# Compress products of the sample sequences' pages: fp32 products replaced by three one-pass products of high and low parts

## What is computed

```
def compress(rows, pe, w1, w2):
    ...
    chunks = rows[:, :n_chunks * CMP_STRIDE].reshape(b, n_chunks, CMP_STRIDE, g, dh)
    ...
    w1_parts = w1.reshape(r, CMP_STRIDE * dh, CMP_HIDDEN)
    pre = pe.reshape(-1) @ w1
    for m in range(r):
        pre = pre + jnp.einsum("bngf,fh->bngh", chunks[:, m:m + n_cmp], w1_parts[m])
    return jax.nn.gelu(pre) @ w2

def nsa_sample(...):
    kcc = compress(history(pool_ck, kc), pe[0], w1[0], w2[0])
    vcc = compress(history(pool_cv, vc), pe[1], w1[1], w2[1])
    o_cmp, p = cmp_attention(q, kcc, vcc, pos)
    idx, ok = select_blocks(p, pos, n_slc)
    ...  # selected_attention over the 16 best blocks, window_attention over the last 512 rows
```

## Time and profile before

| | us |
|---|---|
| median of 3 runs | 1987.12 (1981.58 to 1989.87) |
| the profiled execution, its own time | 1985.21 |
| its span, first to last instruction | 1983.6 |
| PE busy | 1827.7 (92%) |
| DVE, ACT, POOL busy | 898.8, 610.4, 369.0 |
| attention of the prompt, 8 rounds | about 925 to 1116 of the span |
| the four pairs | 1116.8 to 1487 of the span |

### The profile page before, as it was taken

The page is one execution under the profiler, slowest core; times in us unless marked ns, Lnnn a source line. Parts: engine busy times, 40 slices in busy tenths (PEclk is TensorE's granted clock), DMA queues, the critical chain, the costliest instruction groups (busy, mean ns, idle before and its releaser), DMA issues. The chain is left out here.

```text
span 1983.6 us, 33847 instructions
## 1 busy us (share of the span) xinstructions
PE 1827.7 (92%) x12814; PEld 1560.1 (79%) x12814; DVE 898.8 (45%) x1320; ACT 610.4 (31%) x1073; POOL 369.0 (19%) x580
## 2 busy tenths in 40 slices
PE   8999787999999998997888999998988799999996
PEld 8999667999999988995555444444448799999996
DVE  3353287444544434225777340404046644544434
ACT  3222223333332222233666421212123333333222
POOL 0004414000000220020000435343433200000122
PEclk9999679999999998996999999999998899999998
DMA  6222021222223322250000377676643122222331
GB/s 266 85 74 65 28 75 57 91 91 85 85 84 90 89 83 107 85 164 1 1 1 1 97 243 241 222 258 211 212 137 110 56 94 85 85 90 89 88 88 46
DMA packets 89322, 206.15 MB, mean 104 GB/s; under 512 B 13289, under 2 KB 50698, under 8 KB 88466
## 3 DMA queue, kind: packets, MB, share of 16 engines
q1 hardware_dynamic: 71426, 145.00, 22.8%
q0 software_dynamic: 16800, 54.76, 8.3%
q10 hardware_dynamic: 1008, 5.16, 0.6%
HBM read 188.10 MB, written 16.76 MB: 103 GB/s over the span
## 5 line engine op out<-in xcount | busy, mean ns | idle before, releaser
L1230 PE MATMUL ps<-x_parts,piece_parts 128*128 128x272 f32 x6528 | 838.3, 291 | 42.8 <-DVE x_parts L1819 35.0
L1230 PEld LDWEIGHTS ps<-x_parts,piece_parts 128*128 128x128 f32 x6528 | 830.8, 191 | 48.2 <-issue 26.0
L1618 DVE TENSOR_TENSOR piece_parts<-ring,piece_parts 128x1024 fp32r<-128x1024 f32 (+1 forms) x200 | 244.4, 1222 | 617.4 <-ACT piece_parts L1449 617.4
L1449 ACT ACTIVATE piece_parts<-ring 128x1024 fp32r<-128x1024 f32 (+1 forms) x200 | 208.6, 1043 | 584.6 <-PE ps L1230 563.0
L1230 PE MATMUL ps<-big_parts,piece_parts 128*128 128x272 f32 x2176 | 337.2, 291 | 10.6 <-DVE big_parts L1098 6.6
L1230 PEld LDWEIGHTS ps<-big_parts,piece_parts 128*128 128x128 f32 x2176 | 299.9, 192 | 11.9 <-issue 6.8
L659 PE MATMUL ps<-slots,big 128*128 128x512 f32 x512 | 223.9, 595 | 1.6 <-POOLq L1122 1.4
L659 PEld LDWEIGHTS ps<-slots,big 128*128 128x128 f32 x512 | 96.0, 190 | 119.5 <-issue 117.8
L1230 PE MATMUL ps<-hidden_parts,piece_parts 128*128 128x272 f32 x704 | 145.2, 288 | 0.0
L1230 PEld LDWEIGHTS ps<-hidden_parts,piece_parts 128*128 128x128 f32 x704 | 110.7, 189 | 0.0
L1954 POOL COPY slots<-slots 128x2 f32 (+1 forms) x44 | 21.5, 488 | 463.0 <-ACT slots L1578 463.0
(11 more groups left out here) (299 smaller groups left out, 1716.6 us busy)
## 6 DMA issues: line engine op xcount, KB each, us to landing
ring<-in_w_up SPq DMA_DIRECT2D x88, 512.0 KB, 3.3
ring<-in_w_in SPq DMA_DIRECT2D x48, 512.0 KB, 3.4
ring<-in_w_down SPq DMA_DIRECT2D x32, 512.0 KB, 3.5
slots<-in_cmp_k SPq DMA_DIRECT2D x128, 128.0 KB, 3.0
slots<-in_cmp_v POOLq DMA_DIRECT2D x128, 128.0 KB, 2.5
slots<-in_slc_k SPq DMA_DIRECT2D x128, 128.0 KB, 4.1
slots<-in_slc_v POOLq DMA_DIRECT2D x96, 128.0 KB, 2.6
ring<-in_w_out SPq DMA_DIRECT2D x16, 512.0 KB, 3.4
```

The lines of the kernel that those rows point to most:

```text
L1230: mm = pe.matmul(ps[:, 2 * psum_set + h, 0:HT], split[:, slot % 2, w_part, k * 128:(k + 1) * 128], rhs(k)[v_part][:, h * HT:(h + 1) * HT], ...
L1449: act.activation(split[:, s % 2, 0, 0:size], raw[s][:, 0:size], ACT.Copy).then_inc(w_hi, 1)
L1618: ve.tensor_tensor(split[:, s % 2, 1, 0:size], raw[s][:, 0:size], as_f32(split[:, s % 2, 0, 0:size]), ALU.subtract).then_inc(w_lo, 1)
```

## The change

- **compress**: for every chunk column c (8 in each compress), the page rows of 128x512 are divided. ACT copies them to one of four buffers `chunk_hi` in fp32r (`high`), DVE subtracts and writes the low part over the rows in their slot (`low`). PE makes 6 one-pass products: w1_h and w1_l times high for both parts, then w1_h times low for both parts. It waits for `chunk_high` ahead of the first and for `chunk_low` ahead of the fifth. ACT waits for `chunk_free`, which PE raises with the fifth product of a chunk, and which starts at 4. ACT takes over the wait for the pages (`slot_in`).
- **w1** is divided once, in 8 pieces of 128x512, one in each round of the prompt's attention: ACT's copy after ta(3), DVE's subtraction at the round's end. The high part is put where `xls` lay. So DVE first adds `xhs` and `xls` to one row of x in each round (`whole_row`, 128x544), and the layer norm after `out1` reads that sum (one instruction of DVE for a row instead of two). PE waits for `w1_lo` ahead of the first compress.
- **PE's order**: cv0 is cut at chunks 4 and 6 instead of by parts. Chunks 0 to 3 stand after k20, 4 and 5 after k21, 6 and 7 after sc.
- ACT's 32 and DVE's 32 new instructions in a pair are spread by hand between the old ones.
- The buffers lie where the first piece of `out1`, the gate weights and the prompt's masks lay. DVE's loop over the pairs is now three rounds and one written out.

The diff, cut to its core:

```diff
+            pe.sem_inc(chunk_free, 4)
-                    for part in parts:
-                        dst = ps[:, 2 * b + part, :].rearrange("p (g pg n) -> p pg g n", g=4, pg=NPG)
-                        for c in range(8):
-                            mm = pe.matmul(dst, w1[:, v, (part * 8 + c) * 128:(part * 8 + c + 1) * 128], rows[:, :, c, :, :],
-                                           start=c == 0, stop=c == 7)
+                    for c in cs:
...
+                        pe.wait_ge(chunk_high, n)
+                        for part in range(2):
+                            pe.matmul(dst[part], w1_h[:, v, wc[part]], high, start=c == 0, stop=False)
+                            pe.matmul(dst[part], w1_l[:, v, wc[part]], high, start=False, stop=False)
+                        pe.wait_ge(chunk_low, n)
+                        pe.matmul(dst[0], w1_h[:, v, wc[0]], low, start=False, stop=c == 7).then_inc(chunk_free, 1)
+                        mm = pe.matmul(dst[1], w1_h[:, v, wc[1]], low, start=False, stop=c == 7)
...
-                        compress(1, 0, (0,))
+                        compress(1, 0, range(4))
+                compress(1, 0, range(4, 6))
...
-                compress(1, 0, (1,))
+                compress(1, 0, range(6, 8))
...
+                    if u == 3:
+                        act.wait_ge(x_whole, R + 1)
+                        act.activation(w1_h_pieces[:, bass.ds(R, 1), :], w1_pieces[:, bass.ds(R, 1), :], ACT.Copy).then_inc(w1_hi, 1)
...
+            def high(r, name, *cs):
...
+                for c in cs:
+                    if c == 0:
+                        act.wait_ge(slot_in[sl], 384 * r + 256 if sl == 3 else 256 * (1 + 2 * r))
+                    act.wait_ge(chunk_free, 32 * r + (CHUNKS[name] + c + 1))
+                    act.activation(chunk_hi[c % 4], rows[:, c, :, :], ACT.Copy).then_inc(chunk_high, 1)
...
+                high(r, "ck0", *range(8))
+                high(r, "ck1", 0, 1, 2, 3)
+                first(0, ("ck1", 4, 5))
+                high(r, "ck1", 6, 7)
+                high(r, "cv0", 0, 1, 2, 3)
                 first(1)
+                high(r, "cv0", 4, 5, 6, 7)
+                high(r, "cv1", 0, 1)
...
+                high(r, "cv1", 2, 3)
                 first(2)
+                high(r, "cv1", 4, 5)
...
+                high(r, "cv1", 6)
...
+                high(r, "cv1", 7)
                 first(3)
...
+                ve.wait_ge(w1_hi, R + 1)
+                ve.tensor_tensor(w1_l_pieces[:, bass.ds(R, 1), :], w1_pieces[:, bass.ds(R, 1), :],
+                                 as_f32(w1_h_pieces)[:, bass.ds(R, 1), :], ALU.subtract).then_inc(w1_lo, 1)
+                if not last:
+                    whole_row(R + 1)
...
+            def low(r, name, *cs):
+                low_rows, rows = chunk_rows(slots_low, name), chunk_rows(span(F, SLOTS_AT, 4 * 4096), name)
+                for c in cs:
+                    ve.wait_ge(chunk_high, 32 * r + (CHUNKS[name] + c + 1))
+                    ve.tensor_tensor(low_rows[:, c, :, :], rows[:, c, :, :], as_f32(chunk_hi[c % 4]), ALU.subtract).then_inc(chunk_low, 1)
...
-                    ve.scalar_tensor_tensor(out=half(y[:, m, :]), in0=half(as_f32(xhs[:, m, :])), scalar=float(ALPHA), in1=pset(m),
+                    whole = x_rows if r == 2 else as_f32(xhs)
+                    ve.scalar_tensor_tensor(out=half(y[:, m, :]), in0=half(whole[:, m, :]), scalar=float(ALPHA), in1=pset(m),
```

## The result

The changed kernel takes 1960.49 us (median of 4 executions, 1958.39 to 1965.89) against 1984.35 (1981.04 to 1989.87) before: a ratio of 0.9879, 95% interval 0.9856 to 0.9901. That is 24 us less. The forecast was 1942.5, or 44.6 us less; the time lies in the range of 1930 to 1964, at its upper end. The profiled execution took 1962.13 us with a span of 1960.5, so 23.1 us less than the one before. One execution of a later run (the kernel before with one edit) took 3594 us where its five others took 1964 to 1973, and is left out of its figures. About half of the expected gain is missing, and this part is about where it went.

A forecast was written before the change was run, and what follows sets the result against it. PE was taken as the bound, over half of each pair being compress products. Terms -55.4 + 1.4 - 3.4 + 2.8 (ranking) + 3.4 + 2.0 + 4.6 = -44.6 us took 1985.2 to 1940.6; 1.9 for the median gave 1942.5, range 1930 to 1964.

The forecast's parts named there:

- The products: Compress products in the four pairs: 192 one-pass products of 0.2165 us replace 128 of 0.433 a pair, -55.4 us.
- stalls at cv1: PE waits for cv1's chunks 6 and 7, 0.5 and 0.3 us a pair: +3.4 us for four (0 to +5).
- weight loads show: Rival, chance 0.08: a compress product takes 0.225 us, as one-pass products show 12 ns more; kernel at 1949 us.
- Kcc's wait: PE's 0.85 us wait ahead of sc is filled by two chunks of cv0: -3.4 us for four pairs.
- Start of pair 0: ACT's table load now stands ahead of the first chunk copy, so PE starts later: +1.4 us.
- The pages: PE reaches slc_k's loads behind J sooner and may wait: 0 to 2.4 us a pair, 0.5 taken, +2.0 us.
- second rival: Pages late, chance 0.10: DMA engines set slc_k's end, 2.4 us a pair, +7.6 on the forecast, 1950 us.
- The prompt's attention: DVE's two new instructions at each round's end delay the next round: 0.65 us at seven boundaries, +4.6 us (+2.5 to +10).
- Behind cv1: From cv1's end all stays as it was, with the same DMA wait of about 3 us for slc_v.
- The low parts beside POOL: Rival, chance 0.07: DVE's subtractions slow to 1.67 us beside POOL for half the chunks, +24 us, 1966 us.
- PE at its lower clock for all compress products: Rival, chance 0.03: waits idle PE often enough that its clock falls, 166 us on top, 2109 us.
- 131 ns a product: Rival, chance 0.01: compress products come closer than one column a tick, pairs lose 66 us more, 1877 us.

The follow-up runs named there:

- the kernel before with one edit: Kernel before the change, its slc_v products waiting for the other sample's half only ahead of the ninth of sixteen steps: median 1970.7 us, ratio 0.9918.
- divided wait and late window: Changed kernel, waiting for slc_v's second half only before the ninth step, and issuing the window's loads behind cv0's chunk 3: 1945.81 us, ratio 0.9805.

## Why the prediction was right and wrong, point by point

- **The number.** 1960.49 lies in the range, 18 us above the forecast, and partly by luck: the high end of 1964 was added up from 6.5 us for the product's price, 7.6 for the pages, 5.4 for the prompt and some clock, while the product's price alone cost 13.1. Pairs came 83.8 to 88.2 us apart, not 79 to 80.
- **The products: the term that was mis-sized.** Forecast -55.4 us with 0.2165 us for a product (and +3.4 for stalls at cv1, so -52.0); measured -36.6. 768 x (0.2335 - 0.2165) = 13.1 us are the product's price alone; the low clock at pair 0's start adds 2.7, and the first product of each of the twenty stretches takes 0.1 us more, some 2 in all; fewer stalls at cv1 give 2.2 back. The step that failed is the reading of the earlier trace rows: 0.125 us for 272 columns was split into one column a tick and "12 ns that look like a weight load". Read as a price per column, 0.46 ns, it gives 0.235 us for 512, within 1% of what came. Both readings fit the one row; I wrote the additive one down as the upper bound, 0.225. The rival *weight loads show* named too small a price and the wrong cause. The pass of 0.2165 us in the earlier trace rows is half of a two-pass product, and that isn't a one-pass product.
- **cv1's stalls** are 0.3 us a pair, not 0.85. The low clock at pair 0's first products I had not counted.
- **Kcc's wait** went as said: -3.8 for -3.4. **Start of pair 0**: +1.4 as said; 2.81 us of waiting in place of 1.40.
- **The pages.** The forecast left open whether issue (31.7 us after the pair's start) or the DMA engines (38.6) set their end, and took 0.5 of at most 2.4 us a pair. It was the engines: L730 started 38.9 to 40.2 us after the start. My reason for the small 0.5 was the step that failed here. I took the share of 0.77 early in the pair for room, but later in the same stage the engines of the kernel before were full:

```profile
1323.90:1326.90 3.00, 3.00 (x8) 1.33 (x7) 0.00 (x0) 0.00 (x0) 2.84 (x5) 1.00 1.07 364
1329.90:1332.90 3.00, 3.00 (x8) 1.33 (x7) 0.00 (x0) 1.12 (x1) 0.00 (x0) 1.00 1.02 379
```

  From J to cv1 the sum was +4.8, it measured +9.1, between the forecast and its second rival (+12.4). The ranking did run on under the wait, as said, which capped it; what the cap left out is the lower clock behind the longer idle time, 5.7 us in L730 (L743, the window's scores, gets 1.5 us of such a loss back).
- **The prompt's attention**: +4.6 (2.5 to 10) forecast; the stage itself is 5.7 us longer in the first pair of profiles and 7.0 in the mean of all. The named cause, also that PE's idle time lowers its clock more often, held.
- **Behind cv1** I put 0, and it is +3.9: the same wait, with the lower clock behind it in three pairs.
- **The rivals.** The low parts beside POOL took 689 ns: no contention, as the rows on DMA issue said (by columns L1780's rate is 1.66 us for 512, not 1.67, which changes nothing). PE at its lower clock for all compress products didn't happen; 14 products of 768 ran there. 131 ns a product, the distance that the Trainium skill gives in TensorE: Matmul & The Clock Gate, section Back-to-back issue gap, is not what these products do: 0.234 us. The prediction saw the trace agree with the 216 ns of an isolated one, but that was half of a two-pass product; the one-pass product lies 8% above it.

## What to carry to other kernels

Where an engine that bounds a stage gets faster by several us, look up when each transfer of that stage lands, counted from its start: a transfer that ended just ahead of its reader becomes the bound, and the reader then often pays in clock too (5.7 us here). Ask of each wait for several pieces whether the first product needs all of them (15 to 16 us here, from one moved line). And put added instructions into a wait of their engine that the trace shows, not at a loop's end: that place alone was worth 5 to 9 us.

## What the runs showed of the hardware that was not expected

- A one-pass fp32r product costs some 0.45 ns a column and 5 ns besides at a granted clock of 1.00 (0.234 us for 512, 0.12 for 256, 0.125 for 272), while each of the two instructions of an fp32 product of 512 takes 0.433, 0.2165 for a pass. At the lower level the same product is at one column a tick. The changed kernel's first products of pair 0, twelve distances between these two:

```profile
1121.89 0.63 PE L680 MATMUL ps<-chunk_hi,big_parts 128*128 128x512 f32 x1
...
1127.01 0.58 PE L680 MATMUL ps<-chunk_hi,big_parts 128*128 128x512 f32 x1
```

  That is 0.427 us, 512 columns at 1.2 GHz. So the higher level makes them 1.83 times as fast, not twice.
- Products with 64 weight columns whose outputs lie on different halves of the partitions run side by side when they alternate: sixteen fp32 products of 512 columns in 3.65 us, eight in 3.65 when they don't.
- A wait didn't lower the clock by its length alone: behind 2.5 us for `slc_k` (changed kernel, third pair) sixteen products took 5.34 us, behind 2.6 us (divided wait and late window, pair 0) 3.65.
- 1.4 us of DVE at a round's end, eight rounds, moved the mean granted clock of a stretch of 161 us from 0.94 to 0.90 or below; the same work in DVE's wait left it at 0.94.
